# Preparing the output projection during the last head of each mixer

## What is computed

```python
for i in range(DEPTH):                       # 2 layers
    hn = rmsnorm(x, norm_mix[i])
    if i % N_MIXERS == 0:                    # layer 0; y = o.reshape(B, T, GDN_VW) @ w_out
        y, cb, S = gated_deltanet(hn, conv0[j], S0[j], gdn_w_in[j], ..., gdn_w_out[j], L)
    else:                                    # layer 1; y = hc @ w_out
        y, C, n, m = mlstm(hn, C0[j], n0[j], m0[j], ml_w_in[j], ..., ml_w_out[j], L)
    x = x + y
    x = x + swiglu(rmsnorm(x, norm_ffn[i]), ffn_w_gu[i], ffn_w_down[i])
```

## Time and profile before

| | |
|---|---|
| median of 3 runs | 3458.34 us (3452.13 to 3461.75) |
| profiled execution, its own time | 3459.31 us |
| its span, first to last instruction | 3457.6 us |
| PE busy | 3205.4 us, 93% |
| DVE, ACT, POOL busy | 43%, 25%, 35% |
| mean granted TensorE clock | 0.968 |

### The profile page before, as it was taken

The page is one execution under the profiler, slowest core; times in us unless marked ns, Lnnn a source line. Parts: engine busy times, 40 slices in busy tenths (PEclk is TensorE's granted clock), DMA queues, the critical chain, the costliest instruction groups (busy, mean ns, idle before and its releaser), DMA issues. The chain is left out here.

```text
span 3457.6 us, 56187 instructions
## 1 busy us (share of the span) xinstructions
PE 3205.4 (93%) x20698; PEld 3103.9 (90%) x20698; DVE 1484.5 (43%) x2856; ACT 859.7 (25%) x1809; POOL 1209.3 (35%) x1042
## 2 busy tenths in 40 slices
PE   5999999999985999999999979999859999999998
PEld 5889889888875999999999969999859999999997
DVE  4465556555543443333333343334325333333334
ACT  2343443443343121110111124444422110111012
POOL 3333333233313534434443152131153434443430
PEclk8999999999987999999999989999979999999999
DMA  3000100100002111111111020010031111111111
GB/s 128 25 10 25 28 21 8 28 22 9 20 3 77 56 43 55 42 49 37 54 43 48 25 69 20 20 38 20 14 112 43 44 48 38 53 45 46 39 34 50
DMA packets 206958, 137.46 MB, mean 40 GB/s; under 512 B 32121, under 2 KB 198833, under 8 KB 206577
## 3 DMA queue, kind: packets, MB, share of 16 engines
q1 hardware_dynamic: 206832, 135.63, 13.5%
HBM read 120.98 MB, written 14.63 MB: 39 GB/s over the span
## 5 line engine op out<-in xcount | busy, mean ns | idle before, releaser
L89 PE MATMUL ps<-act_hi,ffn_hi 128*128 128x352 f32 x2496 | 813.3, 326 | 60.8 <-POOL ffn_lo L145 59.1
L91 PE MATMUL ps<-act_hi,ffn_lo 128*128 128x352 f32 x2496 | 806.9, 323 | 0.0
L90 PE MATMUL ps<-act_lo,ffn_hi 128*128 128x352 f32 x2496 | 806.0, 323 | 0.0
L143 POOL TENSOR_TENSOR ffn_hi<-ffn_stage,one 128x512 fp32r<-128x512 f32 x296 | 319.4, 1079 | 1034.2 <-PE ps L91 898.5
L89 PEld LDWEIGHTS ps<-act_hi,ffn_hi 128*128 128x128 f32 x2496 | 472.5, 189 | 65.6 <-issue 54.0
L90 PEld LDWEIGHTS ps<-act_lo,ffn_hi 128*128 128x128 f32 x2496 | 474.1, 190 | 0.6
L91 PEld LDWEIGHTS ps<-act_hi,ffn_lo 128*128 128x128 f32 x2496 | 472.6, 189 | 0.0
L145 POOL TENSOR_TENSOR ffn_lo<-ffn_stage,ffn_hi 128x512 fp32r<-128x512 f32 x296 | 406.4, 1373 | 23.2
L900 POOL TENSOR_TENSOR gdn_mt_level<-gdn_mt,joins 128x384 f32<-128x384 f32 x168 | 178.4, 1066 | 595.9 <-DVE gdn_qd L1339 304.7
L730 DVE TENSOR_TENSOR x<-x,ps 128x352 f32<-128x352 f32 x528 | 273.2, 521 | 212.9 <-PE ps L91 212.9
L90 PE MATMUL ps<-ffn_hid_lo,ffn_hi 128*128 128x352 f32 x1056 | 341.7, 324 | 0.0
(11 more groups left out here) (296 smaller groups left out, 5393.3 us busy)
## 6 DMA issues: line engine op xcount, KB each, us to landing
ffn_stage<-in_ffn_w_gu SPq DMA_DIRECT2D x88, 512.0 KB, 3.9
ffn_stage<-in_ffn_w_down SPq DMA_DIRECT2D x44, 512.0 KB, 3.5
gdn_stage<-in_gdn_w_in SPq DMA_DIRECT2D x32, 512.0 KB, 4.3
x_kept<-x SPq DMA_DIRECT2D x2, 4224.0 KB, 12.7
x<-x_kept SPq DMA_DIRECT2D x6, 1408.0 KB, 7.6
ml_stage<-in_ml_w_in SPq DMA_DIRECT2D x16, 512.0 KB, 4.5
load_rows<-in_x_prompt SPq DMA_DIRECT2D x8, 512.0 KB, 4.6
ffn_stage<-in_gdn_w_out SPq DMA_DIRECT2D x8, 512.0 KB, 4.3
```

Source lines behind the costliest of these rows:

```text
L89: pe.matmul(out, w_hi, rhs_hi, start=first, stop=False)
L90: pe.matmul(out, w_hi, rhs_lo, start=False, stop=False)
L91: return pe.matmul(out, w_lo, rhs_hi, start=False, stop=last)
L143: nc.gpsimd.tensor_tensor(hi, st, one, ALU.mult).then_inc(self.hi_done, 1)
```

## The change

The high and low parts of the head outputs, the fetch of x and the first four blocks of `w_out` move from the start of each ffn phase into the last head of the mixer before it.

- ACT makes the high part of one head's output (`high(k)`, 128x1056) at seven places of head 7 for k = 0 to 6; POOL makes the low part (`low(k)`); SP fetches block k of x when its low part is done (`fetch(k)`). Block 7 is split by ACT and DVE per unit at the phase's end (`own_high`, `own_low`); its x is fetched at the start of the ffn phase.
- Two stage slots and two slots of split weights (`KEPT = 2`) now stay allocated over the phases. SP loads blocks 0 and 1 of `w_out` early in head 7; POOL splits them (`OVER_WEIGHTS` in gdn; at the end of its stream in ml); then SP loads blocks 2 and 3 into the freed stages. The ffn phase begins with blocks 0, 1 split and 2, 3 staged.
- In gdn, the transposes and copies of `tails` and their stores move from behind head 7 to ahead of it. In ml, the two stores of m move to ahead of head 7's store.

```diff
+KEPT = 2
 class WeightStream:
-        self.stage = buf("stage", [P, stages, KB, P], F32)
...
+        self.stage = slots(tk.w_stage, "stage", stages, F32)
+        self.hi = slots(tk.w_hi, "hi", ring, F32R)
+        self.lo = slots(tk.w_lo, "lo", ring, F32R)
...
-        pool.sem_inc(self.split_done, self.stages)
+        pool.sem_inc(self.split_done, self.stages + self.ahead)
+        if self.ahead:
+            pool.sem_inc(self.hi_done, 2 * self.ahead)
...
-        pool.wait_ge(self.landed[stage_slot], landed_count)
+        if landed_count is not None:
+            pool.wait_ge(self.landed[stage_slot], landed_count)
...
+class HandOver:
+    HEADS_BEFORE = HEADS - 1
...
+    def high(self, k):
+        self.nc.scalar.copy(self.tk.hi[:, k], self.tk.x[:, k]).then_inc(self.hi_done, 1)
+    def low(self, pool, k):
+        pool.wait_ge(self.hi_done, k + 1)
+        self.nc.gpsimd.tensor_tensor(self.tk.lo[:, k], self.tk.x[:, k], self.tk.hi[:, k].bitcast(F32),
+                                     ALU.subtract).then_inc(self.lo_done, 1)
+    def fetch(self, sp, k):
+        sp.wait_ge(self.lo_done, k + 1)
+        sp.dma_start(self.tk.x[:, k], self.tk.x_dram[:, k]).then_inc(self.x_back, 16)
...
+    def own_high(self, n):
+        k, cols = self.HEADS_BEFORE, unit_cols(n)
+        self.nc.scalar.copy(self.tk.hi[:, k, cols], self.tk.x[:, k, cols]).then_inc(self.own_hi_done, 1)
+    def own_low(self, dve, n):
+        k, cols = self.HEADS_BEFORE, unit_cols(n)
+        dve.wait_ge(self.own_hi_done, n + 1)
+        self.nc.vector.tensor_tensor(self.tk.lo[:, k, cols], self.tk.x[:, k, cols], ...
 def out_ffn_phase
-            for m in range(2):
-                ws.load(sp, m, m, w[:, :, m * P:(m + 1) * P])
-            for n in range(NU):
-                sp.wait_ge(o_lo_done, n + 1)
-                sp.dma_start(x[:, :, unit_cols(n)], tk.x_dram[:, :, unit_cols(n)]).then_inc(x_in[n], 16)
-            for m in range(2, KB):
+            sp.dma_start(x[:, KB - 1], tk.x_dram[:, KB - 1]).then_inc(x_in, 16)
+            for m in range(2 * KEPT, KB):
                 ws.load(sp, m, m % 2, w[:, :, m * P:(m + 1) * P])
...
-            for m in range(KB):
-                ws.split(pool, m, m % 2, m // 2 * 16 + 16, m)
+            for m in range(KEPT, KB):
+                ws.split(pool, m, m % 2, (m // 2 - 1) * 16 if m >= 2 * KEPT else None, m)
...
             for n in range(NU):
-                pe.wait_ge(o_lo_done, n + 1)
                 for m in range(KB):
                     out_tile(n, m)
...
-            for n in range(NU):
-                nc.scalar.copy(tk.hi[:, :, unit_cols(n)], x[:, :, unit_cols(n)]).then_inc(o_hi_done, 1)
...
-            for n in range(NU):
-                dve.wait_ge(o_hi_done, n + 1)
-                nc.vector.tensor_tensor(tk.lo[:, :, unit_cols(n)], x[:, :, unit_cols(n)],
-                                        tk.hi[:, :, unit_cols(n)].bitcast(F32), ALU.subtract).then_inc(o_lo_done, 1)
 def gdn_phase
+    OVER_WEIGHTS = {(0, 5): (0,), (1, 5): (1,)}
+    OVER_LOW = {(0, 6): (0,), (1, 6): (1, 2), (2, 6): (3, 4, 5, 6)}
...
-            head(HEADS - 1, 0)
             for g, dst in enumerate((a["p_conv"], a["s_conv"])):
                 sp.wait_ge(tails_copied, g + 1)
...
+            for m in range(KEPT):
+                ws.load(sp, HEADS * B + m, m, over.weights(m))
+            for m in range(KEPT, 2 * KEPT):
+                ws.load(sp, HEADS * B + m, m % 2, over.weights(m))
+            for k in range(over.HEADS_BEFORE):
+                over.fetch(sp, k)
+            head(HEADS - 1, 0)
...
+                        if ahead == 0:
+                            for m in OVER_WEIGHTS.get((r, l), ()):
+                                pool.wait_ge(unit_done, HEADS * U - NU * (1 - m))
+                                ws.split(pool, HEADS * B + m, m, HEADS * 32 + 16, m)
+                            for k in OVER_LOW.get((r, l), ()):
+                                over.low(pool, k)
...
+            pe.wait_ge(frames_taken, HEADS * 9)
+            pe.wait_ge(evacuated, HEADS * U + 2)
+            for g in range(2):
+                pe.transpose(ps[0:R, g, 0:P], tails[:, g].rearrange("p f h -> p (f h)"), tk.ident[:]).then_inc(tails_turned, 1)
             head(HEADS - 1, False, True)
...
+            for n in range(NU):
+                act.wait_ge(final_done, (HEADS - 1) * 3 + n + 1)
+                over.own_high(n)
...
+            for n in range(NU):
+                over.own_low(dve, n)
+            dve.wait_ge(over.own_lo_done, NU)
 def mlstm_phase
-            head(HEADS - 1, 0)
             sp.wait_ge(pro.step, 56)
...
+            for m in range(2 * KEPT):
+                sp.wait_ge(ws.split_done, HEADS * B + (m + 1 if m < KEPT else m + 2))
+                sp.sem_inc(ws.checked, 1)
+                sp.dma_start(ws.stage[m % 2], over.weights(m)).then_inc(ws.landed[m % 2], 16)
+            for k in range(over.HEADS_BEFORE):
+                over.fetch(sp, k)
+            head(HEADS - 1, 0)
             sp.wait_ge(s_out, HEADS * 64 + 64)
...
+            for m in range(KEPT):
+                pool.wait_ge(unit_done, (HEADS - 1) * U + NU * (m + 1))
+                ws.split(pool, HEADS * B + m, m, HEADS * (32, 16)[m] + 16, m)
+            for k in range(over.HEADS_BEFORE):
+                over.low(pool, k)
```

More of the change, by code:

```diff
@@ L103, with __init__, slots @@
 class WeightStream:
-    def __init__(self, nc, tk, ctx, sem, name, ring, stages=2):
-        self.nc, self.ring, self.stages, self.one = nc, ring, stages, tk.one
-        buf = lambda s, *a: ctx.enter_context(nc.sbuf_tensor(f"{name}_{s}", *a))
-        self.stage = buf("stage", [P, stages, KB, P], F32)
-        self.hi = buf("hi", [P, ring, KB, P], F32R)
-        self.lo = buf("lo", [P, ring, KB, P], F32R)
+    def __init__(self, nc, tk, ctx, sem, name, ring, stages=2, ahead=0):
+        self.nc, self.ring, self.stages, self.one, self.ahead = nc, ring, stages, tk.one, ahead
+        def slots(kept, s, count, dt):
+            own = count - KEPT
+            more = ctx.enter_context(nc.sbuf_tensor(f"{name}_{s}", [P, own, KB, P], dt)) if own else None
+            return [kept[:, i] for i in range(KEPT)] + [more[:, i] for i in range(own)]
+        self.stage = slots(tk.w_stage, "stage", stages, F32)
+        self.hi = slots(tk.w_hi, "hi", ring, F32R)
+        self.lo = slots(tk.w_lo, "lo", ring, F32R)
         self.landed = [sem(f"w_landed{s}") for s in range(stages)]
@@ L836, in gdn_phase @@
         o_normed, final_done = sem("o_normed"), sem("final_done")
+        over = HandOver(nc, tk, sem, a["gdn_w_out"][0])
         block = ctx.enter_context(nc.Block())
@@ L878, in _ @@
                 sp.dma_start(dst[0, 0].rearrange("f (r c) -> (f r) c", c=P), tail_rows[0:R, g]).then_inc(tails_out, 16)
+            for m in range(KEPT):
[5 more added lines that the diff above has]
+            head(HEADS - 1, 0)
             sp.wait_ge(s_out, HEADS * 32 + 32)
             sp.wait_ge(tails_out, 32)
+            over.fetched(sp)
+            for slot in ws.landed:
+                sp.wait_ge(slot, HEADS * 32 + 32)
         @block.gpsimd
@@ L1085, in _ @@
                 o_sums(HEADS - 1, n)
-            pe.wait_ge(frames_taken, HEADS * 9)
-            pe.wait_ge(oln_done, HEADS * 3)
-            for g in range(2):
-                pe.transpose(ps[0:R, g, 0:P], tails[:, g].rearrange("p f h -> p (f h)"), tk.ident[:]).then_inc(tails_turned, 1)
         @block.scalar
@@ L1229, in head @@
                             o_square(t - 1, u)
+                        for k in OVER_HIGH.get((r, l), ()) if not more else ():
+                            act.wait_ge(unit_done, HEADS * U)
+                            act.wait_ge(final_done, (k + 1) * 3)
+                            over.high(k)
                         if more and (r, l) == (2, 2):
@@ L1432, in _ @@
                 head(t, True, True)
+            for g in range(2):
+                dve.wait_ge(tails_turned, g + 1)
+                nc.vector.tensor_copy(tail_rows[0:R, g], ps[0:R, g, 0:P]).then_inc(tails_copied, 1)
             head(HEADS - 1, False, True)
@@ L1899, in head @@
                             chunk(t, r - 1, i)
+                        for k in OVER_HIGH.get((r, i), ()) if not more else ():
+                            act.wait_ge(unit_done, HEADS * U)
+                            act.wait_ge(final_done, (k + 1) * 3)
+                            over.high(k)
                         if (r, i) == (2, 0):
```

77 lines of the change are left out of this document (47 added, 30 removed).

## The result

The changed kernel takes 3408.43 us in the median (3405.01 to 3411.61), the kernel before beside it 3455.54; the ratio is 0.9861 (95% interval 0.9842 to 0.9881). The forecast was 3413 in a range of 3406 to 3425, faster. The profiled execution took 3406.97 us, with a span of 3405.3, 52.3 less than before; the sum had said 45.7.

What follows compares the result with a forecast made beforehand. PE, busy 93% of the span, was taken as the bound, stalled mainly at the two ffn starts. Gains of 21.7 and 24.0 us, total 45.7, from 3459.3 gave 3413.6, or 3412.6 for a median: forecast 3413, range 3406 to 3425.

Steps and rivals of the forecast that it cites:

- the sum: Whole kernel: 21.7 us gained up to unit 0's end in ffn0 and 24.0 in ffn1, total 45.7 us.
- Unit 0: First unit of each ffn phase: ends 33.6 us after the phase's start instead of 58.3 (ffn0) and 58.6 (ffn1).
- POOL's lead: In unit 0: two blocks of split weights ahead of PE, shrinking 0.9 us a tile, last just for eight tiles.
- gdn's last head: Head 7 of gdn gets 4.0 us longer: high parts 1.9, tails 1.0, one collision 1.1.
- the collision: In gdn's last head: DVE and POOL block each other once, costing 1.1 us; none and four as ends.
- The rival built on it: In gdn's last head: three finishes each meet a low part, losing 7.7 us instead of 1.1; time 3420.
- The high parts in batch 2: In gdn's last head: ACT's high parts delay copies PE waits for by about 0.6 and 1.1 us.
- The tails: Put ahead of gdn's last head, they make PE wait for the last evacuation: about 1.0 us with two transposes.
- The ends of the phases: Ends of gdn and ml: ffn0 starts at 1096.1, three us later than before; ffn1 1.0 later, at 2527.8.
- The landing: At ml's end: the store `out_s_n` ends the phase, still 12.8 us after its issue.
- slow low parts: Rival: POOL's low parts take 4.36 us, ffn1 starts 12.3 us later; time 3427; chance 0.12 of 3420 to 3430.
- m did not end ml: Rival at ml's end: the store of m ended ml, so ffn1 starts 5.4 us better; 3408; chance 0.06.

Runs made afterwards that it cites:

- one part alone: The changed kernel with only its weights' part, 3438.45 us (3428.42 with block 4's load earlier), or only its activations' part, 3432.56 us.
- second profile: The unaltered changed kernel, run and profiled once more: 3411.71 us, ratio 0.9867, span 3410.5 us.
- other places: The changed kernel with five high parts and the first low parts moved to later places in gdn's last head: one run of 3411.03 us.
- both edits: The changed kernel with ml's last store split (prompt's state earlier) and gdn's high and low parts at later places: 3400.59 us, ratio 0.9836.
- the activations alone: The changed kernel, but with all blocks of w_out loaded and split in the ffn phase: 3432.56 us, ratio 0.9920.
- the weights alone: The changed kernel, but with head outputs split and x fetched at each ffn phase's start: 3438.45 us, ratio 0.9940.
- other stores: The changed kernel with ml's final stores altered: m behind head 7's store, 3406.64 us; prompt's state earlier, 3402.52; n as rows, with gdn's later places, 3401.56.
- m last: The changed kernel with the two stores of m issued behind head 7's store again, as in the kernel before: 3406.64 us, ratio 0.9849.
- the prompt's state first: The changed kernel with the prompt's state in ml's last head stored ahead of SP's sixth fetch, the sample's at the old place: one run of 3402.52 us.

## Why the prediction was right, step by step

**Unit 0.** Forecast 33.6 us from the phase's start, measured 33.9 and 33.3, and 33.7 and 33.3 again. In ffn0 its parts hold one by one: start at once, about 6 us at the lower clock, 3.87 us a tile, POOL's lead just lasting. In ffn1 two of them missed and made up for each other: 28 matmuls instead of 20 in the first 6.0 us, and so PE came to the last block before POOL had it, 29.0 us after the phase's start (forecast 28.4), and lost 0.7 us. With this lead a quicker PE would not end unit 0 much earlier. The runs with one part alone show that both parts are needed. One cover that the prediction named only for the loads turned out larger: x's fetch, left in the phase, costs 5 us by its place on SP alone.

**gdn's last head.** Forecast +4.0, measured -0.8 in the first profile and +1.3 in the second. The sum had no term for the granted clock, which was 0.83 in this head before, and 0.90 and 0.87 after; in a profile alone the cost can't be told from it. By steps of equal clock: the collision, forecast 1.1, is there and costs 1.1. The last level of batch 0 on DVE in the kernel before:

```profile
1009.97 0.55 DVE L1363 TENSOR_TENSOR gdn_z<-gdn_z,ps 128x384 f32<-128x384 f32 x1
...
1012.81 0.55 DVE L1361 TENSOR_TENSOR gdn_z<-gdn_z,ps 128x384 f32<-128x384 f32 x1 [1.16 <-PE ps L1000]
```

The same level in the changed kernel, with POOL's low part and DVE's finish, and then another low part with a subtraction that reads PSUM:

```profile
1011.18 0.55 DVE L1429 TENSOR_TENSOR gdn_z<-gdn_z,ps 128x384 f32<-128x384 f32 x1
...
1012.11 2.70 POOL L184 TENSOR_TENSOR act_lo<-x,act_hi 128x1056 fp32r<-128x1056 f32 x1
...
1012.64 2.56 DVE L1455 TENSOR_TENSOR x<-x,gdn_o 128x352 f32<-128x352 f32 x1
1015.12 0.54 DVE L1427 TENSOR_TENSOR gdn_z<-gdn_z,ps 128x384 f32<-128x384 f32 x1
...
1042.12 4.79 POOL L184 TENSOR_TENSOR act_lo<-x,act_hi 128x1056 fp32r<-128x1056 f32 x2
...
1043.58 0.55 DVE L1427 TENSOR_TENSOR gdn_z<-gdn_z,ps 128x384 f32<-128x384 f32 x1 [2.06 <-PE ps L1059]
```

The finish takes 2.56 us instead of 0.53, and ends 0.4 us behind the low part in which it started; the subtraction takes its usual 0.55. This is what the Trainium skill says of two SBUF inputs against a PSUM input (SBUF — State Buffer, Who interferes with whom). The rival built on it needed three such meetings; one came, and what three would have cost no run shows. The high parts in batch 2, forecast 1.9 with those of the other batches, cost 1.4 there (1.2 in another run): the copy that PE waits for stands right behind one.

```profile
1059.27 1.05 ACT L180 CAST act_hi<-x 128x1056 fp32r<-128x1056 f32 x1
1060.23 0.47 ACT L1244 COPY gdn_wz<-ps 128x384 f32<-128x384 f32 x1
```

The tails, forecast 1.0, are within the 0.7 us of the runs at the clock of before. Together that is 2.6 to 3.2 us instead of 4.0. An estimate from whole heads agrees in the main: the run with other places and that with both edits have the same gdn code and took 105.4 us at 0.84 and 96.9 at 0.98, so 0.01 of mean granted clock is worth about 0.6 us, and at the clock of before the two profiles of the changed kernel would be 3 to 4 us longer than the kernel before. So the cost was forecast about right, a little too high, and what the profiles show in its place is the clock.

**The ends of the phases.** gdn's: forecast 2.97 us from finish to start, measured 3.16. ml's: forecast 1.0 later, measured 1.2 earlier. That step failed in its sizes. ACT's high parts (0.5 us in the sum) did not delay the store: from head 6's store to head 7's, at a granted clock of 0.82, are 49.3 us in the kernel before, 49.3 in the first profile, 49.1 with the activations alone and 49.2 with the weights alone, which has no high parts there. The fetch (0.5 us) held it for 0.3 us in the first profile and not at all in the second. The landing, which the sum left as it was, took 13.7 us from the start of the issue in the kernel before and 12.4 after (the 12.8 of the prediction counts from the issue's end; so counted, 13.1 and 11.8). As it varies by more than that from head to head, I read this gain as luck. What ends the phase was right, and the runs with other stores show it by moving it. Of the rivals, slow low parts did not come (2.40 to 2.75 us each in the last heads), and m did not end ml.

**The sum.** Of the 6.6 us by which the first profile beat it, 4.8 are the last head and 2.2 the end of ml; the stages around them moved by -2.9, -0.7 and +3.8. In the second profile the same stages moved by +1.0, +2.8 and -0.3. I read these as the span between two runs of one kernel. In the first profile the tile behind DVE's reductions in unit 2 came 0.8 us earlier in both phases; in the second it did not, so that is not the change's either. The medians differ by 47.1 us, and by 45.3 beside the second profile, which is as near to 45.7 as these runs can tell. That nearness is in part luck: unit 0 and the end of gdn came out as summed, the cost of gdn's head was about 1 us too high, the end of ml 2.2 us too late, and stages that the change does not touch moved by up to 3.8 us.

## What to carry to other kernels

Where a phase begins with work for its first matmul, ask for each engine what it must have done and at which pace it then supplies: PE's start, POOL's lead and the transfer of x were three limits, one behind the other, and each shows only when the one ahead is gone. Work that is moved under another phase is paid for at the few instructions that stand right behind it, so look for engine waits of its length, and not for engine idle time in the sum. In gdn's last head the high parts of batch 2 cost 1.2 to 1.4 us ahead of copies that PE waited for; behind other copies they cost nothing that could be seen. A write that the next phase does not read can still end a phase.

## What the runs showed of the hardware

The length of gdn's last head goes with the granted clock in it (and with the few us of work that the variants differ by), and that clock differs from run to run: 96.94 us at 0.98, 101.8 at 0.93, 104.0 to 104.5 at 0.89 to 0.90, 104.2 to 106.1 at 0.87, 104.7 to 105.4 at 0.83 and 0.84. Kernels that are alike there (the changed one, that with m last and that with the prompt's state first) were at 0.90 and 0.87, 0.93, and 0.87. What makes it differ no run here shows. A term of a few microseconds in such a stage can only be read by steps at equal clock, or between windows of equal clock.

A store of 64 elements of 4 bytes from 64 partitions took 11.7 to 12.8 us from its issue to its last landing in the last heads of the changed kernels; the same numbers as one row held SP for 0.7 us. With the other such store 3.5 us ahead the landing was 11.7 and 12.2 us after the issue, with it 1.3 us ahead 12.3 to 12.6: the distance between the two changed it by less than a microsecond.
